# Value products of two attentions, by pairs of heads with 256 moving columns

## The reference

```python
s = jnp.einsum('bqhd,bhkd->bhqk', qi, kt).astype(jnp.float32) * scale
p = jax.nn.softmax(s, axis=-1).astype(vt.dtype)
return jnp.einsum('bhqk,bhkd->bqhd', p, vt)
```

## Time and profile before

| | |
|---|---|
| median of three runs | 1065.82 us (1065.64 to 1067.22) |
| profiled execution, its own time | 1069.91 us |
| span from the first to the last instruction in it | 1068.1 us |
| PE busy | 1048.2 us (98%) |
| DVE busy | 779.7 us (73%) |
| ACT busy | 552.6 us (52%) |
| mla attention, first transposes to the projection | 117.2 to 145.5 us |
| na attention, the same | 796.2 to 849.5 us |
| mean granted clock of PE, of full speed | 0.990 |

### The profile page before, as it was taken

How to read it: one execution, slowest core, us unless ns; L and a number is a source line. 1 busy time by engine, 2 the same in 40 slices (tenths; PEclk the granted TensorE clock), 3 DMA queues, 4 the chain that set the end, 5 groups by cost and what they waited for, 6 DMA issues and landing times.

```text
span 1068.1 us, 20130 instructions
## 1 busy us (share of the span) xinstructions
PE 1048.2 (98%) x7862; PEld 950.1 (89%) x7862; DVE 779.7 (73%) x1381; ACT 552.6 (52%) x951; POOL 115.7 (11%) x133
## 2 busy tenths in 40 slices
PE   6999999999999999999999999999999999999998
PEld 1887787999999989888999999888866799999998
DVE  2697777788887678847677775697439877777876
ACT  4646766444344485555445444546337665454442
POOL 2200012000000037410000000400331020000000
PEclk9999998999999999999999999999999999999999
DMA  9982274989898726465787775387550054656551
GB/s 361 410 315 93 76 246 181 345 344 337 330 354 319 272 64 253 138 255 204 274 288 273 280 269 207 111 291 261 135 99 31 4 187 146 197 166 206 166 189 41
DMA packets 68593, 232.83 MB, mean 218 GB/s; under 512 B 12144, under 2 KB 12432, under 8 KB 68144
## 3 DMA queue, kind: packets, MB, share of 16 engines
q1 hardware_dynamic: 62496, 227.20, 59.6%
q0 software_dynamic: 5888, 3.73, 1.6%
q10 hardware_dynamic: 144, 1.05, 0.3%
HBM read 230.85 MB, written 1.05 MB: 217 GB/s over the span
## 4 chain that ended last, share of the span: by engine, by line
PE 88%; DVE 5%; DMA 3%; issue 2%; ACT 1%; SPq 0%; DVEq 0%; ACTq 0%
PE bank L1902 26%; PE bank L1904 25%; PE bank L1903 25%; PE bank L2427 3%; PE bank L1929 2%; DMA w_raw<-weights 2%; DMA a_raw<-ada 2%; PE bank L2060 2%; DVE bank L1332 1%; PE bank L2069 1%; PE bank L2083 1%; PE bank L1986 1%; DVE w_lo L1205 1%; PE bank L1958 1%; PE bank L2309 1%
## 5 line engine op out<-in xcount | busy, mean ns | idle before, releaser
L1902 PE MATMUL bank<-h_hi,w_hi 128*128 128x256 f32 (+2 forms) x1408 | 404.8, 288 | 3.4 <-DVE h_lo L1853 1.7
L1904 PE MATMUL bank<-h_hi,w_lo 128*128 128x256 f32 (+2 forms) x1408 | 401.7, 285 | 0.0
L1903 PE MATMUL bank<-h_lo,w_hi 128*128 128x256 f32 (+2 forms) x1408 | 401.1, 285 | 0.0
L1205 DVE TENSOR_TENSOR w_lo<-w_raw,w_hi 128x1024 fp32r<-128x1024 f32 x271 | 327.6, 1232 | 64.8 <-ACT w_hi L703 63.4
L703 ACT CAST w_hi<-w_raw 128x1024 fp32r<-128x1024 f32 x271 | 275.5, 1045 | 65.2 <-PE bank L1904 56.8
L1902 PEld LDWEIGHTS bank<-h_hi,w_hi 128*128 128x128 f32 x1408 | 267.5, 190 | 11.4 <-issue 5.2
L1903 PEld LDWEIGHTS bank<-h_lo,w_hi 128*128 128x128 f32 x1408 | 268.0, 190 | 1.3 <-issue 0.2
L1904 PEld LDWEIGHTS bank<-h_hi,w_lo 128*128 128x128 f32 x1408 | 268.0, 190 | 1.0
L1902 PE MATMUL bank<-g_hi,w_hi 128*128 128x256 f32 x528 | 148.9, 282 | 0.0
L1904 PE MATMUL bank<-g_hi,w_lo 128*128 128x256 f32 x528 | 148.8, 282 | 0.0
L1903 PE MATMUL bank<-g_lo,w_hi 128*128 128x256 f32 x528 | 148.7, 282 | 0.0
(11 more groups left out here) (210 smaller groups left out, 1241.0 us busy)
## 6 DMA issues: line engine op xcount, KB each, us to landing
w_raw<-weights SPq DMA_DIRECT2D x281, 512.0 KB, 4.9
a_raw<-ada SPq DMA_DIRECT2D x140, 512.0 KB, 5.4
vals<-ada SPq DMA_DIRECT2D x4, 512.0 KB, 8.7
a_raw<-rpb POOLq DMA_DIRECT2D x9, 224.0 KB, 14.7
bias<-rpb POOLq DMA_DIRECT2D x7, 224.0 KB, 8.2
xT<-xt SPq DMA_DIRECT2D x1, 1024.0 KB, 9.5
big<-ctx SPq DMA_DIRECT2D x1, 1024.0 KB, 14.3
big<-ctx ACTq DMA_DIRECT2D x1, 1024.0 KB, 8.0
```

What stands on the lines that cost most here:

```text
L1205: nc.vector.tensor_tensor(w_lo[:, s, :], w_raw[:, s, :], w_hi[:, s, :].bitcast(fp), SUB)\
L1902: nc.tensor.matmul(out, a_hi, b_hi, start=start, stop=False)
L1903: nc.tensor.matmul(out, a_hi, b_lo, start=False, stop=False)
L1904: return nc.tensor.matmul(out, a_lo, b_hi, start=False, stop=stop)
```

## The change

`weigh` now takes a pair of heads at once: 256 moving columns (both query halves of a head) against the same weights, 8 program products for a pair instead of 16, after steps 2, 4, 6, ... and after the last step. It waits for all four copies of the pair. `probT` becomes two places of one pair each. The first is the room that the two old places had; the second lies in `w_raw`, slots 1 and 2 (`spare` = (15 + 4) % 6 = 1). So SP may load the block that takes slot 1 after an attention (`W_OUT0 + LEAD` and `W_OUT2 + LEAD`) only when all value products of that attention are done, and what stands behind it in SP's list comes later too. Before tile 4 is copied, ACT waits until the blocks before the projection's first are split. `ADA_ISSUED` puts the modulation blocks up to 40 ahead of block 19. Lines in the changed file are 7 to 9 higher.

```diff
 def ada_issue_table():
     at = {RING + n: 17 + n for n in range(4)}
-    at.update({14: 21, 17: 23, 18: 25, 19: 28, 20: 30, 21: 37, 22: 38, 23: 39, 24: 40, 25: 44, 35: 48})
+    at.update({14: 21, 17: 23, 18: 25, 19: 40, 25: 44, 35: 48})
...
-        probT = work[:, PROBS * 512:].rearrange("p (b e k t) -> p b e k t", b=2, e=2, k=4)
+        by_pair = lambda a: a.rearrange("p (t e k q) -> p t e k q", t=2, e=2, k=4)
+        spare = (W_OUT0 + LEAD) % RING
+        probT = [by_pair(work[:, PROBS * 512:]), by_pair(w_raw[:, spare:spare + 2, :].rearrange("p s b -> p (s b)"))]
+        assert spare == (W_OUT2 + LEAD) % RING and spare + 1 < RING
...
             def load_w(w, s):
 
+                if w == W_OUT0 + LEAD:
+                    sp.wait_ge(pv_done, MLA_H)
+                if w == W_OUT2 + LEAD:
+                    sp.wait_ge(pv_done, MLA_H + NA_H)
...
                 def turned(n):
                     if name == "na" and n % 4 == 3:
                         return
+                    if n == 4:
+                        act.wait_ge(split_done, splits_to(w_next - 1))
                     b = wait_tile(act, (name, "tr", n))
                     j, e = n // 2, n % 2
-                    if j >= 2:
-                        act.wait_ge(pv_done, at0 + 2 * (j - 1))
-                    nc.scalar.copy(probT[:, j % 2, e, :, :], b[:, :].rearrange("p (k q) -> p k q", k=4))\
+                    if j >= 4:
+                        act.wait_ge(pv_done, at0 // 2 + 2 * (j // 2 - 1))
+                    nc.scalar.copy(probT[j // 2 % 2][:, j % 2, e, :, :], b[:, :].rearrange("p (k q) -> p k q", k=4))\
                         .then_inc(pT_ready, 1)
...
-                def weigh(j):
-
-                    p, t = j // 2, j % 2
-                    if j == 0:
+                def weigh(p):
+
+                    if p == 0:
                         pe.wait_ge(v_ready, values_ready)
-                    pe.wait_ge(*turned_by(name, at0, 2 * j))
-                    pe.wait_ge(*turned_by(name, at0, 2 * j + 1))
-                    b = write_tile(pe, (name, "o", p)) if t == 0 else bank[tiles[(name, "o", p)][0]]
+                    for n in range(4 * p, 4 * p + 4):
+                        pe.wait_ge(*turned_by(name, at0, n))
+                    b = write_tile(pe, (name, "o", p))
                     for kt in range(4):
                         for e in range(2):
-                            ins = nc.tensor.matmul(b[e * VH:(e + 1) * VH, t * P:(t + 1) * P], values(2 * p + e, kt),
-                                                   probT[:, j % 2, e, kt, :], start=(kt == 0), stop=(kt == 3))
+                            out = b[e * VH:(e + 1) * VH, 0:T].rearrange("p (t q) -> p t q", t=2)
+                            ins = nc.tensor.matmul(out, values(2 * p + e, kt), probT[p % 2][:, :, e, kt, :],
+                                                   start=(kt == 0), stop=(kt == 3))
...
-                    if j:
-                        weigh(j - 1)
-                weigh(heads - 1)
+                    if j and j % 2 == 0:
+                        weigh(j // 2 - 1)
+                weigh(heads // 2 - 1)
```

More of the change, by code:

```diff
@@ L1351, in turned @@
                     j, e = n // 2, n % 2
-                    if j >= 2:
-                        dve.wait_ge(pv_done, at0 + 2 * (j - 1))
-                    nc.vector.tensor_copy(probT[:, j % 2, e, :, :], b[:, :].rearrange("p (k q) -> p k q", k=4))\
+                    if j >= 4:
+                        dve.wait_ge(pv_done, at0 // 2 + 2 * (j // 2 - 1))
+                    nc.vector.tensor_copy(probT[j // 2 % 2][:, j % 2, e, :, :], b[:, :].rearrange("p (k q) -> p k q", k=4))\
                         .then_inc(pT_other, 1)
@@ L2085, in weigh @@
                             if kt == 3:
                                 ins.then_inc(pv_done, 1)
[L2087 to L2094, removed]
+                    pe.wait_ge(rinv_ready, at0 // 4 + p + 1)
@@ L2096, in attention @@
+                    for n in range(4):
+                        e, t = n % 2, n // 2
+                        ins = nc.tensor.matmul(b[e * VH:(e + 1) * VH, T + t * P:T + (t + 1) * P],
+                                               rinv[:, 4 * p + n:4 * p + n + 1].broadcast_to([P, VH]), ident,
+                                               start=True, stop=True)
+                    ins.then_inc(full_of((name, "o", p)), 1)
                 for j in range(begun, 2):
```

## The result

| | before | changed |
|---|---|---|
| median | 1067.22 us (5 runs, 1065.64 to 1068.99) | 1073.89 us (5 runs, 1070.5 to 1074.59) |
| ratio | | 1.0058, interval 1.0042 to 1.0074 |
| profiled execution, its own time | 1069.91 | 1074.59 |
| its span | 1068.1 | 1072.4 |
| mean granted clock of PE in it | 0.990 | 0.992 |

The kernel is slower, by 6.2 us by the ratio and by 4.7 between the two profiled executions. The forecast was 2.4 later, with a range up to 1071.5. The direction was right and the size was not. "Own time" is the device time of the profiled execution; its span, from the first to the last instruction, is a little shorter.

The account below looks back on a forecast made before the run. PE bounds most of the kernel, DVE na's body. Mla's end 0.95, context load 0.5 and na 1.05, less 0.1 hidden, make 2.4 us later: 1065.8 to 1068.2 us, range 1065.8 to 1071.5.

Parts of the forecast that it names:

- the context load's collision: Behind mla: six late weight blocks collide with the second context's load, 0.5 us more, from 0 to 5.
- the two ends: Ends of mla and na: PE waits uncovered for the last copy and starts cold, 0.76 us later at each.
- in turns: Rival behind mla: queues alternate, context waits 2.6 us instead of 0.5; 4.5 later, 1070.3; context chain over forecast 0.16.
- all six: Rival's extreme behind mla: the context is served behind all six blocks, some 5 us later still, 1072.7; outside the range.
- PE does not wait for weights: After mla and na: late blocks land and are split in time for the projection, cost nothing.
- tile 11's copy: End of mla: tile 13's transposes need the bank ACT's copy leaves at 139.29, so PE is 0.19 later.
- Visits 4 and 8: PE's visits to value products: mla 7 to 4, na 15 to 8, saving 0.8 and 1.0 us of PE's time.
- na's start: Start of na: odd steps' scores stand behind all products of a pair; 0.3 us lost, from 0 to 0.9.
- the rival that PE bounds the bodies: Rival, mla and na bodies: PE's 2.3 us are won, 0.8 faster, 1065.0; not slower or under 1.2 later 0.18.
- Serial products: Rival, value products: heads' records don't pair at 256 columns, 21 us later, 1087; chance 0.03.
- The clock rival: Rival, end of na near 847: PE's idle time lowers its clock, up to 1.7 us more, 1069.9; chance 0.08.
- The 2.3 us: PE alone, mla and na: fewer visits 0.8 and 1.0, wider products 0.5, together 2.3 us less.

Follow-up runs that it names:

- e9: The changed kernel itself, unaltered, run again with more runs: ratio 1.0057 against the kernel before.
- e3: The changed kernel, but ACT issues the load of the second context inside mla, at step 4, not behind mla: ratio 1.0020 against the kernel before.
- e4: The changed kernel, but the last pair of each attention is weighed in two halves of 128 columns: ratio 1.0035 against the kernel before.
- e1: The kernel before with only the changed order of loads, products and copies as before: ratio 1.0026.
- e10: The changed kernel, but SP issues blocks 21 to 24 only when the second context has landed: ratio 1.0061 against the kernel before.
- e11: The same kernel as e1 (the kernel before, only its loads changed), run again for a second trace: ratio 1.0037.
- e2: The changed kernel, but mla's second place lies in the value tensor, and blocks 19 to 24 and the modulation table are as before: ratio 1.0016 against the kernel before.
- e8: e1 (the kernel before with the changed order of loads) with the second context loaded at step 4 of mla: ratio 1.0010 against the kernel before.
- e5: e4 with the first pair of each attention by halves too and the second context loaded at step 4 of mla: ratio 1.0018 against the kernel before.
- e7: e5 with mla's second place in the value tensor and mla's loads as before: ratio 1.0009 against the kernel before.
- e6: The kernel before with only the second context's load issued early, at step 4 of mla: ratio 0.9997.

## Why the forecast was wrong

**The step that failed: the context load's collision, sized 0.5, measured 1.8.** In e9's trace it is 1.5, and with the context early (e3) it is 0. Of the 2.3 us between the forecast (2.4) and the traces (4.7), 1.4 are this term; the two ends make 0.4, the time outside the span 0.4, and the rest cancels but for 0.05. That this chain had no slack, and that it was the most uncertain term (0 to 5), was right. Three things were not. First, I sized it by the row of before (8.0 beside one block) and gave "in turns" only 0.16. The transfers of the changed kernel, first from 147.4 to 151.2 us, then from 151.2 to 155.2 (queue 1 carries blocks, queue 10 the context; packets, MB, share of the 16 engines):

```profile
q1 hardware_dynamic: 372, 1.38, 97.5%
...
q10 hardware_dynamic: 125, 0.99, 62.3%
q1 hardware_dynamic: 150, 0.55, 35.9%
```

And in the kernel before, from 147.5 to 151.5; there the first packet of the context came 1.0 us after its issue at 146.46:

```profile
q10 hardware_dynamic: 123, 0.93, 68.6%
q1 hardware_dynamic: 37, 0.11, 7.5%
```

The context issued at 147.34 moves nothing for 3.9 us, while 1.38 MB of blocks pass. After that the queues take turns, 125 packets to 150, but the context gets through as much in four microseconds as it did before (0.99 MB, 0.93). So the 2.1 us by which it lands later (10.1 for 8.0) come from ahead of its first packet: 2.9 more there, and 0.8 less from there to the landing. Four blocks had been issued ahead of it there, and the first packet came after 3.9 in e4 and e9 too, which have the same four; with two ahead it came after 1.5 to 2.5 (e1, e10, e11), with one modulation block ahead, issued 2.1 and 3.2 us earlier, after 1.0 (before, e2).

That is nearer to a wait behind the blocks issued first, of which the forecast had only the extreme (all six, 5 us), than to turns. The rival "in turns" has the right size, 2.6 for the context, and its sum of 4.5 is near the 4.7 of the traces, but by luck: beside e2, where almost no block's packets ran with the context's and it landed in 6.1, 1.1 of the 4.0 us more lie behind the first packet, where the turns are, and 2.9 ahead of it.

The Trainium skill ("DMA: Bandwidth & Descriptors", section "Queues, rings and completion order") has the rule of turns between queues that have work, and the counts of packets agree with it for the four microseconds after the context's first packet; the 3.9 before it do not follow from the rule, and why a queue should wait so long for its first turn stays open.

Second, the lateness took another way to PE. I followed POOL's sums alone. ACT's list was the shorter way: the squares stand ahead of the split of block 21, DVE's updates of x stand behind that split, and PE needs the banks these empty. Before, the split of block 21 came 0.2 us after the squares without any wait. So one late transfer is paid at a bank (1.1), in a wait of which the forecast's list had nothing, and by DVE's delay once more at the squares (0.7), through the late issue of a weight block.

Third, "PE does not wait for weights" held for the transfers by themselves (e8), but not beside the context: in e1 block 20 was 8.9 on its way where I had counted some 1.3 each in order. In the changed kernel itself PE had no such wait.

**The ends, sized 0.76 each, cost 0.96.** The mechanism was right at both: in e4, where products on tiles copied earlier stand between again, both are back. What was too small is the start behind a wait: 0.25 + 1.95 = 2.20 from the copy's end to the last product, where I had 0.04 + 0.22 + 1.74 = 2.00. The term for tile 11's copy (0.19) was right: mla is later by 0.21 in e4, which has only that left.

**The rest.** Visits 4 and 8, a pair 1.88 behind other work, na's start 0.31 (0.3), na's body unchanged (DVE 6.59 for 6.57): as forecast; the rival that PE bounds the bodies is refuted by e5 and e7, which keep the saved visits and gain nothing. Serial products are refuted by the 1.95. The clock rival did not come: near 853 us the changed trace has no stretch of half clock. After na the loads cost nothing, as I had it (e1 and e11, 0.0 at na's end). The 2.3 us that fewer visits and wider products take off PE alone came back nowhere, since DVE, and ACT behind it, set the pace of both bodies.

**Between 4.7 and 6.2.** Before's 35 runs beside e1 show what the mean clock does: four at 0.998 took 1064.7 to 1065.1, four at 0.990 took 1069.6 to 1070.8, so 0.001 is some 0.7 us (a straight line through all 35 gives 0.6). Beside e9, before's 15 runs had a mean of 0.9961 and the changed kernel's 6 had 0.9938: 1.5 of the 6.1 us. What is left, 4.6, is near what the traces say: the stages that the change touches and the 0.4 outside the span make 4.6 in the first and 4.1 in e9's. Whether the change itself brings the lower clock, or the draw of a few runs did, stays open: e1 and e11 suggest that waits can (below), and e4 had 0.9929 and e10 0.9923, but e2 with the same products had 0.9962.

Open too is the 0.4 outside the span. It is there in each kernel with wide products (2.13 to 2.29 in all their runs) and in none without (1.75 to 1.94), whatever the loads; no view shows what it is.

No version here is faster than the kernel before by more than its interval (the best is e6, 0.9997).

## What to carry to other kernels

Count a change to a matrix engine's list against the engine that feeds it: when the period of the two is within a hundredth, saved gaps are worth nothing, and only what the change uncovers at the first and the last turn shows. When transfers are made to start later, list every other load that then starts beside them, and which of them are issued ahead of it, and follow each of these through the list of the engine that waits for it: what stands behind the waiting instruction (here the split of block 21, which had landed 2.3 us before) may reach the bound sooner than the data itself. And a transfer that can go early, since its room is free, removes such a collision for nothing, even where it gains nothing by itself (e3, e8, e6).

## What the runs showed of the hardware

- Two queues that both have work take nearly equal numbers of packets (125 of 8 KB, 150 of up to 4 KB in 4 us), so the one with the larger packets gets about two thirds of the bytes. But a transfer issued right behind four others on another queue moved its first packet only 3.9 us after its issue (changed, e4, e9), behind two others after 1.5 to 2.5 (e1, e10, e11), with only a single one, issued 2.1 and 3.2 us earlier, after 1.0 (before, e2). In e3, where the issue itself stood 2.63 us in ACT's queue, it came 1.0 after the end of that.
- PE's clock falls to 1.2 GHz in separate stretches, mostly at the same few places (near 22, 46, 173, 375 and 460 us), and each execution has some of them and not others; e6's profiled one had none before 1064 us. This is most of the spread from 1064 to 1071 us between runs of one and the same kernel.
- Behind a long wait of PE a stretch came where no other kernel had one. In e1 and e11 PE waited 2.3 and 2.8 us for DVE, and then (us, busy of PE PEld DVE ACT POOL, clock, DMA, GB/s), e1 and then e11:

```profile
160.00:164.00 4.00, 4.00 (x23) 4.00 (x22) 4.00 (x7) 1.91 (x3) 3.84 (x3) 0.57 0.71 222
```

```profile
159.00:166.00 7.00, 6.14 (x29) 6.14 (x30) 7.00 (x10) 3.64 (x6) 6.69 (x6) 0.51 0.58 182
```

In the changed kernel, with a wait of 1.1, there was none at this place.
